# First two row tiles of the output projection dealt into the last 22 decode pieces, prompt rows loaded later, on one Trainium2 core

## What is computed

```python
attn = attn_fn(q, k, v, logf)                       # 512 features
rwkv_out, wkv_new = rwkv7_time_mix(...)             # 512 features
mixed = jnp.concatenate([attn.reshape(B, T, FOX_WIDTH).astype(x.dtype),
                         rwkv_out.astype(x.dtype)], axis=-1) @ w_out
h = x + mixed
hn = rms_norm(h, ln2_g)
h = h + (jax.nn.silu(hn @ w_gate) * (hn @ w_up)) @ w_down
y = rms_norm(h, lnf_g)
```

## Time and profile before

| | us |
|---|---|
| Median of 3 runs | 1430.83 |
| The profiled execution | 1438.99 |
| Its span, first to last instruction | 1437.3 |
| TensorE matmuls busy in it | 1335.8 (93%) |
| Mean granted TensorE clock | 0.958 of full |

### The profile page before, as it was taken

One profiled execution on the slowest core, in us unless ns is written; L12 is line 12 of the kernel. 1 busy time (PEld: TensorE's weight loads), 2 busy tenths in 40 slices (PEclk: granted clock), 3 DMA queues, 4 the chain that ended last, 5 costly groups with the idle time before them and its releaser, 6 DMA issues.

```text
span 1437.3 us, 28554 instructions
## 1 busy us (share of the span) xinstructions
PE 1335.8 (93%) x11707; PEld 970.7 (68%) x11707; DVE 565.8 (39%) x1084; ACT 387.5 (27%) x769; POOL 110.8 (8%) x223
## 2 busy tenths in 40 slices
PE   5999999997979999989998787999999999999997
PEld 4754666664557677777774555447777777788886
DVE  5013255554383443434326223145443433363322
ACT  3020233235465444425452453111000000000001
POOL 6373100000000000000300201000000000000000
PEclk8999799998799999999998988999999999999998
DMA  6177210106588777678886989800312311223101
GB/s 216 60 159 192 70 60 1 37 0 230 177 300 310 225 242 254 221 239 267 243 283 199 357 287 352 262 1 10 107 59 61 116 59 59 81 81 121 41 8 59
DMA packets 128843, 219.37 MB, mean 153 GB/s; under 512 B 11483, under 2 KB 46374, under 8 KB 128710
## 3 DMA queue, kind: packets, MB, share of 16 engines
q1 hardware_dynamic: 120818, 193.64, 40.6%
q0 software_dynamic: 7824, 23.85, 6.1%
q10 hardware_dynamic: 68, 0.02, 0.0%
HBM read 203.06 MB, written 14.41 MB: 151 GB/s over the span
## 4 chain that ended last, share of the span: by engine, by line
PE 85%; DVE 5%; ACT 3%; DMA 3%; issue 2%; SPq 1%; POOL 0%; POOLq 0%; DVEq 0%; ACTq 0%
PE PS L1408 21%; PE PS L794 13%; PE PS L1490 9%; PE PS L1236 7%; PE PS L1250 4%; PE PS L1364 4%; PE PS L1295 4%; PE PS L767 2%; DMA out_wkv_prompt<-arena 1%; PE PS L1499 1%; PE PS L1050 1%; PE PS L1054 1%; PE PS L1060 1%; DMA arena<-in_cache_v 1%; PE PS L825 1%
## 5 line engine op out<-in xcount | busy, mean ns | idle before, releaser
L1408 PE MATMUL PS<-arena 128*128 128x288 f32 x1232 | 300.3, 405 | 1.1 <-issue 0.6
L1408 PEld LDWEIGHTS PS<-arena 128*128 128x128 f32 x1232 | 232.5, 189 | 67.9 <-DVE arena L2497 1.0
L794 PE MATMUL PS<-arena 128*128 128x301 f32 (+1 forms) x736 | 198.5, 427 | 0.0
L1760 ACT ACTIVATE arena<-PS 128x512 f32<-128x512 f32 x256 | 141.6, 595 | 171.2 <-PE PS L1236 170.9
L794 PEld LDWEIGHTS PS<-arena 128*128 128x128 f32 (+1 forms) x736 | 137.2, 190 | 54.9 <-issue 14.1
L1236 PE MATMUL PS<-arena 128*128 128x128 f32 x1024 | 153.3, 294 | 20.8 <-ACT arena L1760 7.2
L1236 PEld LDWEIGHTS PS<-arena 128*128 128x128 f32 x1024 | 120.5, 149 | 51.6 <-issue 30.5
L1490 PE MATMUL PS<-arena 128*128 128x256 f32 x616 | 134.4, 379 | 0.0
L1490 PEld LDWEIGHTS PS<-arena 128*128 128x128 f32 x616 | 116.3, 189 | 17.6 <-issue 0.8
L1250 PE MATMUL PS<-arena 128*32 128x128 f32 x2048 | 85.8, 286 | 0.0
L1295 PE MATMUL PS<-arena 128*32 128x256 f32 x1024 | 72.5, 400 | 10.0 <-DMA arena<-in_cache_v 9.3
(11 more groups left out here) (380 smaller groups left out, 1526.3 us busy)
## 6 DMA issues: line engine op xcount, KB each, us to landing
arena<-in_cache_k SPq DMA_DIRECT2D x256, 256.0 KB, 4.2
arena<-in_cache_v SPq DMA_DIRECT2D x256, 256.0 KB, 4.4
arena<-in_w_gate SPq DMA_DIRECT2D x11, 1024.0 KB, 5.6
arena<-in_w_up SPq DMA_DIRECT2D x11, 1024.0 KB, 8.2
arena<-in_w_down SPq DMA_DIRECT2D x8, 1408.0 KB, 6.3
arena<-in_w_in SPq DMA_DIRECT2D x5, 2048.0 KB, 12.5
forgets_after<-arena POOLq DMA_DIRECT2D x64, 128.0 KB, 8.4
arena<-forgets_after SPq DMA_DIRECT2D x32, 256.0 KB, 5.2
```

The lines of the kernel that those rows point to most:

```text
L794: ins = mm(PS[0:width, bank, 0:HALF], wring[:, c % 2, k, c0:c0 + width], xnT[:, k, half * HALF:(half + 1) * HALF], start=(k == 0), stop=(k ...
L1408: ins = mm(PS[:, bank, 0:HO], weights[:, j], moving[:, j], start=(first and j == 0), stop=(j == KH - 1), skip_group_check=not first)
L1760: av(KTs[:, (2 * i + q) % LOT], PS[:, T_USE[("k", L, i, q)] % 2, :].rearrange("p (g n) -> p g n", g=NG), ACT.Copy)\
```

## The change

`project(n)` becomes a generator for the four prompt tiles. Its order inside changes: first the four FoX feature blocks for both halves of the columns, then the four RWKV blocks for both, with the partial sums standing in two PSUM banks meanwhile. It yields after every two feature blocks of one half, so a tile is 8 parts of two block products, and the four tiles 32 parts. Part 1 waits for `wo_in` and for `hs_taken` 16, part 5 (the first with RWKV features) for `rwkv_done`.

From piece 234 on, 14 parts are dealt out over the last 22 pieces: part 1 after piece 235, then one each after pieces 237, 238, 240, 241, 243, 244, 246, 248, 249, 251, 252, 254 and 255. That is all of tile 0 and 6 of the 8 parts of tile 1. Behind the pieces come 2 parts, `turn_probs(31)`, 4 parts, `lot_values(31)`, 4 parts, `turn_output(3)`, and 8 parts. The samples' projection keeps its place and form under the name `project_samples`.

GpSimd, before it loads the prompt rows, also waits for `k_free` to reach 256, which is when TensorE has turned the last keys of lot 30 (piece 245).

VectorE's stream after its lots becomes `add_residual(0)`, `add_sums(31)`, `add_residual(1)`, `norm_rows(0)`, `add_output(31)`, `scale_output(3)`, `norm_rows(1)`, `take_output(3)`, `add_residual(2)`, `weight_sum` as before.

```diff
             pool.wait_ge(S["rwkv_done"], 1)
+            pool.wait_ge(S["k_free"], 2 * LOT * LOTS)
             for i in range(1, NTILE):
                 pool.dma_start(x2[:, i, :], t_in["x_prompt"][0, (i - 1) * P:i * P, :]).then_inc(S["x2_in"], 16)
...
+            def project(n):
+                rows, cols = rows_of(order[n])
+                if n == 0:
+                    pe.wait_ge(S["wo_in"], 16)
+                    pe.wait_ge(S["hs_taken"], 4 * NG)
+                elif n >= 2:
+                    pe.wait_ge(S["h_ready"], n - 1)
+                for features in (range(0, NG), range(NG, KT)):
+                    if n == 0 and features[0]:
+                        pe.wait_ge(S["rwkv_done"], 1)
+                    for half in range(2):
+                        for k in features:
+                            ins = mm(PS[rows, E + 2 * (n % 2) + half, :], mixT[:, k, cols], wo[:, k, half * NB:(half + 1) * NB],
+                                     start=(k == 0), stop=(k == KT - 1), skip_group_check=True)
+                            if k == KT - 1 and half:
+                                ins.then_inc(S["mixed_out"], 1)
+                            if k % 2:
+                                yield
...
+            FIRST_PIECE, N_PARTS = 8 * LOTS - 22, 14
+            projections = itertools.chain(*[project(n) for n in range(NTILE - 1)])
+
+            def projected(piece):
+                return max(0, N_PARTS * (piece + 1 - FIRST_PIECE) // (8 * LOTS - FIRST_PIECE))
+
             rest, done = rwkv_rest(), 0
             for piece, _ in enumerate(all_lots()):
                 while done < rwkv_due(piece):
                     next(rest)
                     done += 1
+                for _ in range(projected(piece) - projected(piece - 1)):
+                    next(projections)
             assert done == N_RWKV and next(rest, 1) == 1
...
-            pe.wait_ge(S["rwkv_done"], 1)
-            pe.wait_ge(S["wo_in"], 16)
-            project(0)
+            def project_parts(n):
+                for _ in range(n):
+                    next(projections)
+
+            project_parts(2)
             turn_probs(LOTS - 1)
-            project(1)
+            project_parts(4)
             for half in range(2):
                 lot_values(LOTS - 1, half)
-            project(2)
+            project_parts(4)
             turn_output(NPAIR - 1)
-            project(3)
+            project_parts(8)
+            assert next(projections, 1) == 1
             pe.wait_ge(S["o_done"], NPAIR)
...
-            project(4)
+            project_samples()
...
+            add_residual(0)
             add_sums(LOTS - 1)
-            add_residual(0)
+            add_residual(1)
+            norm_rows(0)
             add_output(LOTS - 1)
             scale_output(NPAIR - 1)
-            add_residual(1)
-            norm_rows(0)
+            norm_rows(1)
             take_output(NPAIR - 1)
             add_residual(2)
-            norm_rows(1)
             for i in range(4):
                 weight_sum(0, i)
             add_residual(3)
```

More of the change, by code:

```diff
@@ L1344, in _, with rows_of, project_samples @@
             new_scores(0)
+            def rows_of(i):
+                return (slice(64, P), slice(SEQ, OUTC)) if i == 0 else (slice(0, P), slice((i - 1) * P, i * P))
+            order = [1, 2, 3, 4, 0]
+            def project(n):
[16 more added lines that the diff above has]
+                                yield
+            def project_samples():
+                rows, cols = rows_of(0)
+                pe.wait_ge(S["h_ready"], NTILE - 2)
+                for k in range(KT):
+                    for half in range(2):
+                        ins = mm(PS[64 * half:64 * half + 64, E, :], mixT[:, k, cols], wo[:, k, half * NB:(half + 1) * NB],
+                                 start=(k == 0), stop=(k == KT - 1), skip_group_check=True)
+                ins.then_inc(S["mixed_out"], 1)
+            FIRST_PIECE, N_PARTS = 8 * LOTS - 22, 14
+            projections = itertools.chain(*[project(n) for n in range(NTILE - 1)])
+            def projected(piece):
+                return max(0, N_PARTS * (piece + 1 - FIRST_PIECE) // (8 * LOTS - FIRST_PIECE))
             rest, done = rwkv_rest(), 0
@@ L1349, in _ @@
                     done += 1
+                for _ in range(projected(piece) - projected(piece - 1)):
+                    next(projections)
             assert done == N_RWKV and next(rest, 1) == 1
-            def rows_of(i):
-                return (slice(64, P), slice(SEQ, OUTC)) if i == 0 else (slice(0, P), slice((i - 1) * P, i * P))
-            order = [1, 2, 3, 4, 0]
[L1357 to L1371, removed]
-            pe.wait_ge(S["rwkv_done"], 1)
-            pe.wait_ge(S["wo_in"], 16)
-            project(0)
+            def project_parts(n):
+                for _ in range(n):
+                    next(projections)
+            project_parts(2)
             turn_probs(LOTS - 1)
-            project(1)
+            project_parts(4)
             for half in range(2):
                 lot_values(LOTS - 1, half)
-            project(2)
+            project_parts(4)
             turn_output(NPAIR - 1)
-            project(3)
+            project_parts(8)
+            assert next(projections, 1) == 1
             pe.wait_ge(S["o_done"], NPAIR)
```

## The result

The changed kernel takes 1421.97 us (median), the kernel before 1431.80 us beside it. The ratio is 0.9931 with a 95% interval of 0.9910 to 0.9951, so the change saves 7 to 13 us, about 9.9 by the medians.

The account below looks back on a forecast made before the run. TensorE, busy for 93% of the span, was taken as the bound, with only idle and half-clock stretches to win. Page waits and cold clock -11.1, ScalarE waits -0.7, switches +2.1: -9.7 us, 1430.8 to 1421.1 us, range 1416 to 1428.

Parts of the forecast that it names:

- The bound: TensorE, busy for 93% of the span: only its idle and half-clock stretches, just ahead in lot 30, can be won.
- Rival (b): Lot 30's page wait is an accident of the profiled execution; 2 us off either way, 1430 us; chance 0.12.
- The sum: Whole kernel: -11.1 - 0.7 + 2.1 = -9.7 us, from 1430.8 to 1421.1 us.
- The cost of a switch: Parts behind column-tiled products in lots 29 to 31: 0.19 us each, 2.1 us in all; bounds nothing and 5 us.
- Pages in time: Lots 30 and 31: about 17.2 us from slot release to use, so remaining page wait 0, other bound 4 us.
- Rival (a): Pages stay a little late in lot 30, a wait of 4 us in all; 1425.1 us; chance 0.12.
- The move of the rows: Prompt rows' loads moved to piece 245: no cost, little worth with the parts, most of the wait by itself.
- The new waits: TensorE's waits for hs_taken, wo and rwkv_done at parts 1 and 5: none ends last, cost nothing.
- VectorE's order: VectorE's stream after its lots, first residual ahead of add_sums: cost nothing.
- the late weights: Feed-forward weights, issued once the values' slots are freed at about 915, asked for at 938: cost nothing.
- rival (c): Parts in lots 30 and 31 run at the half clock; 15 us slower, 1446 us; chance 0.03.
- gain "elsewhere": A cold stretch elsewhere in the kernel goes too: 2 to 3 us more, 1416 us.

Follow-up runs that it names:

- e12: The kernel before with only the RWKV spread two pieces later; 1427.0 us, 0.9966 of the kernel before.
- e6: The changed kernel with the same 14 parts put behind transposes instead of column-tiled products; 1421.6 us, 0.9929 of the kernel before.
- e9: The changed kernel with the parts behind transposes and the RWKV spread two pieces later; 1414.1 us, 0.9895 of the kernel before.
- e1: The changed kernel without GpSimd's new wait, so prompt rows load at the old place, right behind rwkv_done; 1421.0 us, 0.9918 of the kernel before.
- e11: The changed kernel itself, run again beside other kernels; 1423.3 us, 0.9955 of the kernel before.
- e4: The changed kernel with the rows at the old place and the four prompt tiles loaded a second time; 0.9937 of the kernel before.
- e5: The changed kernel with only 7 parts dealt out, the other 9 of tiles 0 and 1 behind the last piece; 0.9971 of the kernel before.
- e2: The kernel before with only GpSimd's new wait, rows loaded behind the last keys of lot 30; 1.0021 of the kernel before.
- e7: The kernel before with the rows loaded behind the last keys of lot 31, no parts dealt out; 1422.5 us, 0.9933 of the kernel before.
- e8: The changed kernel with the four RWKV steps behind VectorE's reciprocal two pieces later; 1413.4 us, 0.9884 of the kernel before.
- e10: The kernel before with rows behind the last keys of lot 31 and the RWKV spread two pieces later; 1419.0 us, 0.9917 of the kernel before.

## Why the prediction was right, and where it was not

**The bound.** Right. The page waits in lot 30 and the half clock behind them are what the change won, and they are in both profiles of the old arrangement (4.55 and 2.78 us before, 2.22 and 4.18 in e12). Rival (b), an accident of one execution, falls, by these and by 20 timed runs of each kernel. That only idle and half-clock stretches could be won is too narrow: a better order of the same parts took another 3.4 us off the seam (e6, e9).

**The sum.** 9.7 us forecast; 9.74 us at the seam at full clock (e1 and e11 against before), 9.9 us between medians. That they agree to 0.2 us is partly luck: the timed gain has an interval of 7 to 13 us, its repeat in e11 gave 6, and the seam before is that of one execution. From the start of lot 30 to `turn_h` the forecast was 72.8 us, measured 956.12 - 884.25 = 71.9 us.

**The cost of a switch.** 0.19 us taken from the earlier trace rows; measured 1.92 - 1.72 = 0.20 us, for the 12 parts that were named. That a weight load makes it, as the prediction says, was not tested; the trace fits it in part (behind transposes the first load of a part starts 0.11 us ahead of its first product, 885.08 against 885.19, behind values at the same moment, 881.76). Behind a part, values take 1.00 us instead of 0.86, and transposes 0.87 instead of 1.02, four times each, which cancels; the upper bound of 5 us was not needed.

**Pages in time.** Right, with room: e4 adds 5.9 us of DMA time and no wait comes back. Rival (a) was found only where parts were too few (e5).

**The move of the rows.** Half right. With the parts it is worth nothing, as said (88.49 us at the seam in e1 and in e11, the changed kernel at full clock). But the sentence that the move "would take most of the wait by itself" is wrong: e2 gained nothing. The step that failed was to price the pages behind piece 245 only with the parts in place, and for the move alone to look at no pages but those that the rows had delayed so far. By the prediction's own count 2 to 2.5 MB are still to come there, and the toll was paid on them: 9.1 us of page waits in e2's seam, against 7.8 before. Only behind the last key page (e7) does the move work, and then it is worth as much as the parts.

**The new waits, VectorE's order, the late weights.** Cost nothing, as forecast: no row of TensorE names one of them, the first residual starts without a gap, and the time behind `turn_h` is 475.5 us in both.

**The half clock, rival (c).** It did not strike the parts: the clock was 0.99 from 870 us to `turn_h`, and 1.00 over the whole seam in e1 and e11. The full clock forecast from lot 29 on was missed by its first 4 us (3.83 us for sixteen transposes), left over from the stretch ahead. The rule of the Trainium skill (TensorE: Matmul & The Clock Gate, section Loop structure matters more than you think) speaks of waits between matmuls, and parts of a torn contraction without waits between them lost only the 0.20 us a switch. Beyond what lot 30 lost before, the prediction looked for the half clock in the wrong place. It had it as a possible loss in lots 30 and 31, and only as a vague gain "elsewhere"; after the change it lies ahead of the seam, and moved a profile by up to 10.2 us behind the 1.97 us wait, as much as the whole change.

**The profiled execution.** 1429.3 us was forecast, and it was 1433.16. The first RWKV product came 3.2 us earlier than before (846.88 against 850.06), but with the half clock behind it the way to the fourth took 18.13 us instead of 13.52, and the half clock reached 6 us into the seam, which cost 2.45 us. Two profiles are no measurement of a change of 0.7%; the seam, mark to mark, is.

## What to carry to other kernels

When a transfer delays others behind it, moving it back by a step only moves the wait, unless it gets behind the last transfer whose buffer has no lead; so count what is still to come at the new place. Independent matmuls dealt out in small parts hid such a toll at both places where the rows' loads stood, and needed no exact place; have more than enough of them (11.3 us of parts were just too few here, 24 us left room), and put them behind full-width products, which the trace shows to be cheaper and the run times leave open. And when the runs of a kernel scatter by more than a change is worth, compare profiles between two marks around the edit, and look for short waits behind which the clock falls: moving work into one of them gave 2 to 9 us, in four comparisons, though it did not end the scatter.

## What the runs showed of the hardware

A wait of 1.97 us, with one of 1.70 us shortly ahead of it, was followed by anything from no half-clock time at all (e1, e4) to 23.12 us of it at an engine that was busy throughout (after). At half clock the same instructions take about twice as long: the four L913 products 2.50 us instead of 1.34, sixteen key transposes 3.83 us where eight took 1.09. Waits of 1.70 and some 1.46 us, about as close together, were followed by no half-clock time in four profiles (e8, e9, e10, e12). In the profile after, the granted clock stayed at the half for all that time, with TensorE busy for 23.12 of 23.12 us, and was back at 1.00 by 872 us. A software-queue load of 2.88 MB beside the page stream took 14.1 us for its last transfer before and 13.6 us in e1, with and without parts on TensorE.
